# RWKV recurrence of a two-block transformer: levels on half the columns, and the pair blocks masked on three engines

## The reference: what is computed

```python
def wkv7(r, w, k, v, a, b):
    # S_t = S_{t-1} diag(w_t) + (S_{t-1} a_t) b_t^T + v_t k_t^T ;  y_t = S_t r_t
    def step(S, inp):
        r_t, w_t, k_t, v_t, a_t, b_t = inp
        sa = jnp.einsum('bhvk,bhk->bhv', S, a_t)
        S = S * w_t[:, :, None, :] + sa[..., None] * b_t[:, :, None, :] + v_t[..., None] * k_t[:, :, None, :]
        y = jnp.einsum('bhvk,bhk->bhv', S, r_t)
        return S, y
```

## Time and profile before

| | |
|---|---|
| median of 3 runs | 1394.11 us |
| profiled execution, span | 1392.2 us |
| recurrence, from the first mask of unit 0 to the last of unit 7 | 782.1 to 885.7 us |
| TensorE clock granted in it | full in every slice |

### The profile page before, as it was taken

How to read it: one execution, slowest core, us unless ns; L and a number is a source line. 1 busy time by engine, 2 the same in 40 slices (tenths; PEclk the granted TensorE clock), 3 DMA queues, 4 the chain that set the end, 5 groups by cost and what they waited for, 6 DMA issues and landing times.

```text
span 1392.2 us, 23783 instructions
## 1 busy us (share of the span) xinstructions
PE 1362.8 (98%) x8927; PEld 1117.8 (80%) x8927; DVE 855.2 (61%) x1234; ACT 696.6 (50%) x1110; POOL 38.1 (3%) x42
## 2 busy tenths in 40 slices
PE   8999999999999999999999999999999999999998
PEld 7888877778888878888787688778888887788887
DVE  4545577875755464445784788766555677555554
ACT  5444456675465464444554444235444566644442
POOL 0000000000000000000001000110000010000000
PEclk9999999999999999999999999999999999999999
DMA  8655545556444565555352101314555651265552
GB/s 294 214 181 181 181 140 202 167 188 200 161 163 157 148 207 197 189 195 186 115 196 77 61 4 33 112 46 166 181 189 184 227 175 52 83 212 194 182 184 104
DMA packets 145537, 220.25 MB, mean 158 GB/s; under 512 B 16761, under 2 KB 65295, under 8 KB 145329
## 3 DMA queue, kind: packets, MB, share of 16 engines
q1 hardware_dynamic: 145456, 219.14, 47.8%
HBM read 218.04 MB, written 1.05 MB: 157 GB/s over the span
## 4 chain that ended last, share of the span: by engine, by line
PE 88%; DVE 6%; ACT 3%; issue 1%; POOL 1%; DMA 1%; SPq 0%; DVEq 0%; ACTq 0%; POOLq 0%
PE acc L291 12%; PE acc L293 12%; PE gp L291 12%; PE acc L292 12%; PE gp L293 12%; PE gp L292 12%; PE tp L944 1%; PE gp L2767 1%; PE acc L2782 1%; DVE sb_w_lo L280 1%; PE acc L1280 1%; PE tp L291 1%; ACT sb_w_hi L264 1%; ACT sb_arena L407 1%; DMA sb_raw<-in_ffn_w 1%
## 5 line engine op out<-in xcount | busy, mean ns | idle before, releaser
L280 DVE TENSOR_TENSOR sb_w_lo<-sb_raw,sb_w_hi 128x1024 fp32r<-128x1024 f32 (+1 forms) x380 | 451.5, 1214 | 207.4 <-ACT sb_w_hi L264 205.7
L264 ACT ACTIVATE sb_w_hi<-sb_raw 128x1024 fp32r<-128x1024 f32 (+1 forms) x380 | 387.9, 1052 | 210.9 <-PE acc L293 106.9
L291 PE MATMUL gp<-sb_w_hi,sb_xa_hi 128*128 128x512 f32 (+1 forms) x752 | 298.5, 397 | 5.0 <-DVE sb_w_lo L280 3.5
L293 PE MATMUL gp<-sb_w_lo,sb_xa_hi 128*128 128x512 f32 (+1 forms) x752 | 291.7, 388 | 0.0
L292 PE MATMUL gp<-sb_w_hi,sb_xa_lo 128*128 128x512 f32 (+1 forms) x752 | 291.2, 387 | 0.0
L291 PEld LDWEIGHTS gp<-sb_w_hi,sb_xa_hi 128*128 128x128 f32 x752 | 141.3, 188 | 37.8 <-DVE sb_w_lo L280 6.7
L293 PEld LDWEIGHTS gp<-sb_w_lo,sb_xa_hi 128*128 128x128 f32 x752 | 141.2, 188 | 29.6
L292 PEld LDWEIGHTS gp<-sb_w_hi,sb_xa_lo 128*128 128x128 f32 x752 | 141.5, 188 | 27.1 <-issue 0.5
L291 PE MATMUL acc<-sb_w_hi,sb_mid_hi 128*128 128x512 f32 x400 | 156.2, 390 | 0.0
L293 PE MATMUL acc<-sb_w_lo,sb_mid_hi 128*128 128x512 f32 x400 | 155.8, 390 | 0.0
L292 PE MATMUL acc<-sb_w_hi,sb_mid_lo 128*128 128x512 f32 x400 | 155.7, 389 | 0.0
(11 more groups left out here) (417 smaller groups left out, 1756.8 us busy)
## 6 DMA issues: line engine op xcount, KB each, us to landing
sb_raw<-in_ffn_w SPq DMA_DIRECT2D x264, 256.0 KB, 4.3
sb_raw<-in_mlp_w SPq DMA_DIRECT2D x256, 256.0 KB, 2.9
sb_raw<-in_w_in SPq DMA_DIRECT2D x72, 256.0 KB, 3.2
sb_raw<-in_a_w_rkv SPq DMA_DIRECT2D x48, 256.0 KB, 4.1
sb_raw<-in_xattn_w_kv SPq DMA_DIRECT2D x32, 256.0 KB, 3.6
sb_raw<-in_w_out SPq DMA_DIRECT2D x16, 256.0 KB, 3.2
sb_raw<-in_xattn_w_q SPq DMA_DIRECT2D x16, 256.0 KB, 3.1
sb_raw<-in_xattn_w_o SPq DMA_DIRECT2D x16, 256.0 KB, 3.1
```

Source lines behind the costliest of these rows:

```text
L264: A.e.activation(w_hi[:, s, :, 0:n], raw[:, r, :, 0:n], ACT.Copy).then_inc(hi_done, 1)
L280: V.e.tensor_tensor(w_lo[:, s, :, 0:n], raw[:, r, :, 0:n], w_hi[:, s, :, 0:n].bitcast(F32), ALU.subtract).then_inc(lo_done, 1)
L291: e.matmul(dst, xh, wh, start=start, stop=False)
L293: return e.matmul(dst, xh, wl, start=False, stop=stop)
```

## The change

Three things change.

- Each level computes and copies only the half of the columns (32 of 64) in which its mask can be set. At level n the columns fall into blocks of b = 2^(n+1); z and x use the left block of each pair of blocks, y the right one. The product's moving operand is strided (`side`), the result lies packed in PSUM, and the copy scatters it (`sides` from `packed`). `z_buf` gets an identity once per stream, since only half of it is written per level.
- The pair blocks are laid out by kind: banks 0 and 1 (in `acc`) take kinds 0 and 1 of all heads, banks 2 and 3 (in `gp` and `tp`) kinds 2 and 3. VectorE masks only the first two. ScalarE copies the other two unmasked into `mt` (`act_rest`), and GpSimd multiplies them by the mask in place (`pool_rest`).
- In the order, `pe_a_mat` of unit u stands ahead of `pe_rhs` of unit u-1, and `dve_first_y` ahead of `dve_first_x`, which is one instruction and not two.

```diff
+            def side(self, x, b, right):
+                return x.rearrange("p (c h b) -> p c h b", h=2, b=b)[:, :, right, :]
+            def sides(self, x, b, right):
+                return x.rearrange("p m (c h b) -> p m c h b", h=2, b=b)[:, :, :, right, :]
+            def packed(self, x, b):
+                return x.rearrange("p (m c b) -> p m c b", m=4, b=b)
...
-                for j in range(2):
-                    if i and j:
+                for a in range(2):
+                    if i and a:
                         T.e.wait_ge(self.y_done, u - 1)
-                    for a in range(2):
+                    for j in range(2):
                         for e in range(2):
                             part = slice(e * HD, (e + 1) * HD)
-                            mm = T.e.matmul(self.stream_banks(s)[2 * j + e][:, 256 * a:256 * a + 256], fm[part, j, 2 + a, :],
+                            mm = T.e.matmul(self.stream_banks(s)[2 * a + e][:, 256 * j:256 * j + 256], fm[part, j, 2 + a, :],
...
-                        mm = T.e.matmul(gp[there, s, m * HALF:(m + 1) * HALF], self.mt[s][at, m, 0, there], self.x_inv[s][at, m, :], start=True, stop=True)
+                        mm = T.e.matmul(gp[there, s, m * QUARTER:(m + 1) * QUARTER], self.mt[s][at, m, 0, there], self.side(self.x_inv[s][at, m, :], b, 0),
+                                        start=True, stop=True)
...
             def pe_rhs(self, T, u):
                 s, i, t, g = self.place(u)
+                T.e.wait_ge(*stage(self.rest_masked, 2 * u + 2))
...
                     self.pe_z(T, u - 1, 3)
+                    self.pe_a_mat(T, u)
                     self.pe_rhs(T, u - 1)
-                    self.pe_a_mat(T, u)
                     self.pe_xy(T, u - 1, 3)
...
-                A.e.activation(self.z_buf[s].rearrange("p m d -> p (m d)"), gp[:, s, 0:256], ACT.Copy).then_inc(*A.one(self.z_done[s]))
+                A.e.activation(self.sides(self.z_buf[s], 2 ** (n + 1), 0), self.packed(gp[:, s, 0:P], 2 ** (n + 1)), ACT.Copy).then_inc(*A.one(self.z_done[s]))
...
                 for u in range(1, self.UNITS):
+                    self.act_rest(A, u, 0)
                     self.act_z(A, u - 1, 3)
                     self.act_rhs(A, u - 1)
                     self.act_z(A, u, 0)
                     self.act_z(A, u - 1, 4)
+                    self.act_rest(A, u, 1)
                     self.act_z(A, u, 1)
...
+            def act_rest(self, A, u, e):
+                s = u % 2
+                if u == 0:
+                    A.e.wait_ge(self.rows_ready, NT)
+                A.e.wait_ge(*stage(self.pairs_rest, 2 * u + e + 1))
+                A.e.activation(self.pair_blocks(s, 1, e), self.pair_bank(s, 1, e), ACT.Copy).then_inc(*A.one(self.rest))
+            def pool_rest(self, G, u):
+                s = u % 2
+                for e in range(2):
+                    G.e.wait_ge(*stage(self.rest, 2 * u + e + 1))
+                    r = self.pair_blocks(s, 1, e)
+                    G.e.tensor_tensor(r, r, const("upper").rearrange("p (j x) -> p j x", j=2), ALU.mult).then_inc(*G.one(self.rest_masked))
...
-                V.e.copy_predicated(self.x_inv[s], self.four(levels[:, 1, n + 1, :]),
-                                    acc[:, s, 512:768].rearrange("p (m s) -> p m s", m=4)).then_inc(*V.one(self.x_done[s]))
+                V.e.copy_predicated(self.sides(self.x_inv[s], 2 ** (n + 1), 0), self.four(self.side(levels[:, 1, n + 1, :], 2 ** (n + 1), 0)),
+                                    self.packed(acc[:, s, 512:640], 2 ** (n + 1))).then_inc(*V.one(self.x_done[s]))
...
                     self.dve_masks(V, u)
+                    self.dve_first_y(V, u)
                     self.dve_first_x(V, u)
                     if old:
                         self.dve_x(V, u - 1, 3)
-                    self.dve_first_y(V, u)
```

More of the change, by code:

```diff
@@ L75 @@
 HALF = P // 2
+QUARTER = P // 4
 COLUMN_TILES = (slice(0, HALF), slice(HALF, P))
@@ L2275, in pool @@
                 self.pool_rows(G)
-                for n in range(3):
+                for u in range(self.UNITS):
+                    self.pool_rest(G, u)
+                    if u == self.UNITS - 2:
+                        self.pool_gn(G, 0)
+                for n in range(1, 3):
                     self.pool_gn(G, n)
@@ L2752, in pe_a_mat @@
                             part = slice(e * HD, (e + 1) * HD)
-                            mm = T.e.matmul(acc[at, s, e * 512 + j * HALF:e * 512 + (j + 1) * HALF], fm[part, j, 0, there], fm[part, j, 2, at],
-                                            start=True, stop=True)
+                            mm = T.e.matmul(acc[at, s, e * 512 + j * QUARTER:e * 512 + (j + 1) * QUARTER], fm[part, j, 0, there],
+                                            self.side(fm[part, j, 2, at], 1, 0), start=True, stop=True)
                 mm.then_inc(*T.one(self.a_mat))
@@ L2778, in pe_xy @@
                 for m in range(4):
-                    at_m = slice(m * HALF, (m + 1) * HALF)
+                    at_m = slice(m * QUARTER, (m + 1) * QUARTER)
                     if n < LEVELS - 1:
                         for at, there in self.crossed():
-                            mm = T.e.matmul(acc[at, s, 512:1024][:, at_m], self.y_inv[s][there, m, :], self.z_buf[s][there, m, :], start=True, stop=True)
+                            mm = T.e.matmul(acc[at, s, 512:1024][:, at_m], self.y_inv[s][there, m, :], self.side(self.z_buf[s][there, m, :], b, 0), start=True, stop=True)
                         if m == 3:
@@ L2785, in pe_xy @@
                     for at, there in self.crossed():
-                        mm = T.e.matmul(acc[there, s, 0:512][:, at_m], self.z_buf[s][there, m, :], self.y_inv[s][there, m, :], start=True, stop=True)
+                        mm = T.e.matmul(acc[there, s, 0:512][:, at_m], self.z_buf[s][there, m, :], self.side(self.y_inv[s][there, m, :], b, 1), start=True, stop=True)
                 mm.then_inc(*T.one(self.inv_y[s]))
@@ L2939, in act_identity @@
                     A.e.wait_ge(self.u, 2 * (u - 1))
+                if u < 2:
+                    A.e.activation(self.z_buf[s], const("ident64").unsqueeze(1).to_broadcast([P, 4, HALF]), ACT.Copy).then_inc(*A.one())
+                    self.z_whole[s] = A.last
                 for dst in (self.y_inv[s], self.x_inv[s]):
@@ L3017, in dve_first_x @@
                 V.e.wait_ge(self.a_mat, u + 1)
-                for e in range(2):
-                    src = acc[:, s, e * 512:e * 512 + 2 * HALF].rearrange("p (j d) -> p j d", j=2)
-                    V.e.copy_predicated(self.x_inv[s][:, e::2, :], levels[:, 1, 0, :].unsqueeze(1).to_broadcast([P, 2, HALF]), src).then_inc(*V.one(self.first_x))
+                src = acc[:, s, :].rearrange("p (e x) -> p e x", e=2)[:, :, 0:2 * QUARTER].rearrange("p e (j c) -> p e j c", j=2)
+                mask = self.side(levels[:, 1, 0, :], 1, 0).rearrange("p c b -> p (c b)")
+                dst = self.x_inv[s].rearrange("p (j e) (c h) -> p e j c h", e=2, h=2)[:, :, :, :, 0]
+                V.e.copy_predicated(dst, mask.unsqueeze(1).unsqueeze(1).to_broadcast([P, 2, 2, QUARTER]), src).then_inc(*V.one(self.first_x))
             def dve_first_y(self, V, u):
@@ L3025, in dve_first_y @@
                 V.e.wait_ge(self.identity, 2 * (u + 1))
-                V.e.wait_ge(self.masked, 4 * u + 4)
+                V.e.wait_ge(self.masked, 2 * u + 2)
                 for at, there in self.crossed():
-                    V.e.copy_predicated(self.y_inv[s][there], levels[at, 0, 0, :].unsqueeze(1).to_broadcast([HALF, 4, HALF]),
-                                        self.mt[s][at, :, 0, there]).then_inc(*V.one(self.first_y))
+                    V.e.copy_predicated(self.sides(self.y_inv[s][there], 1, 1), self.four(self.side(levels[at, 0, 0, :], 1, 1)),
+                                        self.sides(self.mt[s][at, :, 0, there], 1, 1)).then_inc(*V.one(self.first_y))
             def dve_x(self, V, u, n):
```

35 lines of the change are left out of this document (24 added, 11 removed).

## The result

The changed kernel takes 1402.09 us (median of 4 runs, 1400.34 to 1405.17) against 1394.72 for the kernel before on the same chip: a ratio of 1.0055, 95% interval 1.0043 to 1.0067. It is slower; the forecast was 1387.5, faster. Its profiled span is 1400.8 us, 8.6 more than before.

The account below looks back on a forecast made before the run. TensorE, busy in 98% of the span, was taken as the bound, with the recurrence's chain of waits to shorten. Savings of 6.6 us took the span from 1392.2 to 1385.6, plus 1.9 gives 1387.5; range 1377 to 1398.

Parts of the forecast that it names:

- I take zero: z products on TensorE: no saving from 32 moving columns, since the weights stay 64 wide and so the spacing stays.
- rival 1: TensorE's product groups halve with their columns, 0.24 us less each, 11 to 12 us more saved: 1376; chance 0.12.
- mostly under rhs: If GpSimd delays only first_y on VectorE, the loss is at most one product's time, mostly hidden while TensorE runs rhs.
- Rival 3: GpSimd's products shut VectorE out of SBUF while they run: 1.8 us per unit, 14 in all, 1402; chance 0.10.
- Part 1: a_mat ahead of rhs, two masks fewer: first x/y product 0.54 us earlier after first mask (unit 5: 0.53).
- Part 2: Shorter copies on VectorE and ScalarE: 0.39 us less from a unit's first x/y product to y.
- tails: Last records of TensorE's product groups shrink at hand-overs: 0.5 us over all units.
- Rival 2: Scattered access makes copies on VectorE and ScalarE cost what they did, about 4 us of gain lost: 1391.5; chance 0.13.
- Part 3: Added work per unit, two ScalarE copies of 0.60 us and two GpSimd products of 1.4 us each, costs nothing.
- rival 4: GpSimd takes over 6.7 us per product, so rhs waits; each us above costs 14 in all; chance 0.03.
- rival 5: New order costs elsewhere: late masks make a_mat block rhs, 0.1 us per unit per 0.1 late, 1389 to 1394; chance 0.12.
- The sum: Units 1 to 4 3.7 us, unit 5 1.1, unit 6 0.35, unit 7 0.4, unit 0 0.5, tails 0.5: 6.6 us.

Follow-up runs that it names:

- late product: The changed kernel, with GpSimd's first product of each unit also waiting for first_y so that the two do not overlap: 1392.61 us, ratio 0.9990.

## Why the prediction was wrong

**The step that failed first is a term that the prediction does not have: TensorE's clock.** "I take zero" for the 32 columns rested on the spacing of the products, and the spacing is right: z groups still start 0.46 us apart (862.58 and 863.04 in unit 5), so rival 1 is out. But units 2 and 3 lost 16.84 + 18.35 - 2 x 14.37 = 6.5 us to half clock, and the work behind unit 7 another 512.4 - 509.0 = 3.4. That is 9.9 us together, more than the whole loss of 8.6 in the span. With the same weight loads and half the columns, the chip gave half the clock behind a wait. Neither the wait alone (64 columns, 1.00 us: full) nor the columns alone (late product, units 1 to 6: full) did it in the traces.

**The second step that failed is "mostly under rhs".** Rival 3 was right in kind, and had 0.10. Its price of 1.8 us per unit was too high, since only first_y is blocked; the x and y copies, which read from PSUM, were not touched. Its total of 1402 is the measured time, but that is luck: the clock made up the rest. In the weaker form (only first_y can be hit) the loss was to hide under rhs. In units 1 to 4 rhs covers 0.6 us only, first_y has first_x behind it on VectorE, and z waits. The block costs S 0.78 in unit 4 (4.85 against 4.07), as much as the change earns elsewhere: without it the units are 13.6, with it 14.4.

**Part 1** forecast S = M + 3.94 in units 1 to 4 and M + 4.38 in unit 5. Without the block it is 4.07 and 4.37, but not for the reasons given. In before, S had two causes that end almost together in unit 4, z's copy at 843.12 and first_y, behind four masks, at 843.17:

```profile
842.25 0.92 DVE L3028 COPY_PREDICATED sb_arena<-sb_levels,sb_arena 64x256 f32<-64x256 uint8 x2
842.74 0.38 ACT L2947 ACTIVATE sb_gain_b<-gp 128x256 f32<-128x256 f32 x1 [1.46 <-PE gp L2767]
```

The order alone shortens only the path of z, two masks fewer only that of first_y, and in the runs either alone gives nothing. Part 1 gave 0.54 per unit, 0.10 of it from the copy of z. Of the other 0.44 only 0.17 came from the order and the masks; the rest of what S gained came from the half columns (4.48 to 4.24, where part 1 had the 0.10 of z's copy). VectorE's end of it was mis-sized too: first_x was to end at M + 2.3 and ends at M + 2.8, since the first_y pair takes 0.92 instead of two times 0.3.

**Part 2** forecast 0.39 from S to the next mask; 9.87 became 13.57 - 4.07 = 9.50, 0.37 less. That the two agree is in part luck. The short copies alone give 0.25 (14.00 - 4.38 = 9.62): of the two x copies on the path, that of level 0 keeps its 0.44. The other 0.12 came with the products of 32 columns, to which the prediction gave only "tails", 0.5 us over all units; with the late product 32 columns instead of 64 save 1.1 us from unit 0 to 7 (96.66 against 97.75). ScalarE's z copies take 280 ns at every level, as forecast from the earlier trace rows. VectorE's mean is 321 to 337 instead of 294, since the level 0 copies, in runs of two elements, take 0.44, as the whole ones did. first_x, in single elements, takes 0.44 as well, and halving first_y gave nothing (the pair takes 0.92 in the trace of before as in that with the late product). Rival 2 is right for these.

```profile
L3099 DVE COPY_PREDICATED sb_arena<-sb_levels,acc 128x128 f32<-128x128 uint8 x20 | 6.4, 321 | 0.4 <-PE acc L2808 0.3
...
L2975 ACT ACTIVATE sb_gain_b<-gp 128x128 f32<-128x128 f32 x20 | 5.6, 280 | 17.7 <-PE gp L2787 17.6
```

**Part 3** gave GpSimd's product 1.4 us; it takes 1.28, and rhs never waited for it (rival 4 is out). Masks were ready for a_mat, which starts at M + 1.34 (rival 5 is out in the changed kernel, though the order does cost in units 6 and 7 where it stands alone).

**The sum** of 6.6 us is 4.4 from unit 0 to unit 7 in the kernel with the late product (96.66 us against 101.07): 0.73 to 0.78 for each of units 1 to 4 instead of 0.93, 0.77 for unit 5 instead of 1.1, 0.19 for unit 6 instead of 0.35, 0.39 for unit 0 instead of 0.5. Behind that the late instructions of unit 7 take up to 2.02 us instead of 0.57.

## What to carry over

When a change makes TensorE's products smaller at an unchanged spacing, look for the waits beside them and at the granted clock, and keep the columns wide if the spacing is set by the weights anyway. Before giving GpSimd work on SBUF, list the VectorE instructions with both inputs in SBUF that can run beside it, and what stands behind them; a wait on one semaphore removed the whole price here.

Where two paths end together, neither edit is worth anything by itself, so take a change apart before saying what its parts gave. Here the masks moved to two other engines and the new order, the harder half of the change, earned some 0.4 us of 4.4. A small edit taken alone (the short copies, 0.9979) did as well as the best of the whole.

When a row's releaser reads "issue", look whether the program waits there at all before naming a load, and then at when the queue of kind "instruction" was served.

## What the runs showed of the hardware

- With 32 moving columns against 64 x 64 weights, TensorE ran at 1.2 GHz behind waits or gaps of 0.26, 0.42, 0.74, 1.07 and 1.6 us, for 6 to 15 us at a time, but not behind each of them (0.74 us: units 2 and 3, not 1 and 4). With 64 columns at the same spacing it kept 2.4 GHz behind waits of 0.3 to 1.84 us in the traces, and fell for 3.3 us behind the one of 2.02.
- A GpSimd product of 512 elements takes 1.28 us on 128 partitions, and lengthens a pair of predicated copies with two SBUF inputs from 0.92 to 1.73 us, those from PSUM not at all.
- VectorE's predicated copy of 128 elements takes 0.44 us where they lie in single elements or runs of two, and 0.28 to 0.30 in runs of four and more; ScalarE's copy of 128 takes 0.28 to 0.29 in runs of two as in longer ones.
- TensorE stood still for 0.16 to 2.02 us with nothing waited for in 17 of 20 traces, in unit 5 or 7, and each time went on 1.3 to 1.6 us after a 16 KB packet of the instruction queue had landed.
